# Moving the probability scaling of sparse attention to GpSimd, cutting weight splitting into pieces, and starting the gate products behind the compressed scores

## The reference, cut to what matters

```python
def masked_softmax(s, mask):
    s = jnp.where(mask, s.astype(jnp.float32), NEG_INF)
    return jax.nn.softmax(s, axis=-1) * mask
...
        o_cmp, p_cmp = nsa_compressed(q, kv[:, :, 0], kv[:, :, 1], ...)   # 31 compressed keys
...
    out = lax.map(body, (qb, ib, mb, jnp.arange(nq)))                     # selected and window keys
...
        y = (gm[:, :, 0] * (y_nsa @ w_proj_nsa[l]) + gm[:, :, 1] * (y_ml @ w_proj_ml[l])
             + gm[:, :, 2] * (y_mem @ w_proj_mem[l]))
```

## Time and profile before

| | us |
|---|---|
| median of 3 runs | 2846.68 (2845.8 to 2847.77) |
| the profiled execution's own time | 2845.7 |
| its span | 2843.9 |
| PE busy | 2756.7 (97%) |
| DVE busy | 2074.1 (73%) |
| ACT busy | 1194.7 (42%) |
| POOL busy | 86.9 (3%) |

### The profile page before, as it was taken

The page is one execution under the profiler, slowest core; times in us unless marked ns, Lnnn a source line. Parts: engine busy times, 40 slices in busy tenths (PEclk is TensorE's granted clock), DMA queues, the critical chain, the costliest instruction groups (busy, mean ns, idle before and its releaser), DMA issues.

```text
span 2843.9 us, 41346 instructions
## 1 busy us (share of the span) xinstructions
PE 2756.7 (97%) x16318; PEld 2421.5 (85%) x16318; DVE 2074.1 (73%) x3097; ACT 1194.7 (42%) x1739; POOL 86.9 (3%) x114
## 2 busy tenths in 40 slices
PE   7999898899999999999999999999999999999998
PEld 7888777777888989889898899987999888789897
DVE  4456567676658969589695797875978588669794
ACT  4333455555333434334343444332434357524342
POOL 0000022221000000000000000000000000000000
PEclk9999999999999999999999999999999999999999
DMA  7223313222533332323333233332332343123332
GB/s 221 89 78 104 111 53 93 78 93 84 171 119 104 112 111 95 128 75 115 108 97 98 81 107 109 97 98 91 101 116 93 109 174 121 60 74 104 108 100 74
DMA packets 262207, 295.51 MB, mean 104 GB/s; under 512 B 6210, under 2 KB 248018, under 8 KB 259342
## 3 DMA queue, kind: packets, MB, share of 16 engines
q1 hardware_dynamic: 257008, 281.53, 30.6%
q10 hardware_dynamic: 5022, 11.57, 1.1%
HBM read 276.30 MB, written 16.78 MB: 103 GB/s over the span
## 4 chain that ended last, share of the span: by engine, by line
PE 86%; DVE 8%; issue 3%; ACT 2%; ACTq 0%; DVEq 0%; DMA 0%; SPq 0%
PE bank L1461 14%; PE bank L1462 14%; PE bank L1463 14%; PE bank L1898 8%; PE bank L1896 8%; PE bank L1897 8%; PE bank L1735 3%; PE bank L2059 1%; PE bank L1476 1%; PE bank L1477 1%; PE bank L1478 1%; PE bank L1803 1%; PE bank L1754 1%; DVE probT_low L2451 1%; PE bank L1489 1%
## 5 line engine op out<-in xcount | busy, mean ns | idle before, releaser
L2154 DVE TENSOR_TENSOR w_lo<-w_raw,w_hi 128x2048 fp32r<-128x2048 f32 (+2 forms) x140 | 306.3, 2190 | 139.0 <-ACT w_hi L847 134.1
L847 ACT ACTIVATE w_hi<-w_raw 128x2048 fp32r<-128x2048 f32 (+2 forms) x134 | 243.0, 1820 | 240.9 <-PE bank L1463 162.2
L1461 PE MATMUL bank<-hid_hi,w_hi 128*128 128x512 f32 x880 | 343.0, 390 | 0.0
L1462 PE MATMUL bank<-hid_lo,w_hi 128*128 128x512 f32 x880 | 342.5, 389 | 0.0
L1463 PE MATMUL bank<-hid_hi,w_lo 128*128 128x512 f32 x880 | 342.4, 389 | 0.0
L1461 PE MATMUL bank<-h_hi,w_hi 128*128 128x512 f32 x752 | 298.8, 397 | 3.4 <-DVE w_lo L2154 1.7
L1462 PE MATMUL bank<-h_lo,w_hi 128*128 128x512 f32 x752 | 293.1, 390 | 0.0
L1463 PE MATMUL bank<-h_hi,w_lo 128*128 128x512 f32 x752 | 293.0, 390 | 0.0
L1463 PEld LDWEIGHTS bank<-hid_hi,w_lo 128*128 128x128 f32 x880 | 165.2, 188 | 34.5
L1461 PEld LDWEIGHTS bank<-hid_hi,w_hi 128*128 128x128 f32 x880 | 165.2, 188 | 34.0
L1462 PEld LDWEIGHTS bank<-hid_lo,w_hi 128*128 128x128 f32 x880 | 165.2, 188 | 33.6
(11 more groups left out here) (479 smaller groups left out, 7060.6 us busy)
## 6 DMA issues: line engine op xcount, KB each, us to landing
w_raw<-in_ffn_w_in_dram SPq DMA_DIRECT2D x88, 1024.0 KB, 5.1
w_raw<-in_ffn_w_out_dram SPq DMA_DIRECT2D x32, 1024.0 KB, 5.0
w_raw<-in_w_in_dram SPq DMA_DIRECT2D x28, 1024.0 KB, 5.2
w_raw<-in_w_ffn_in_dram SPq DMA_DIRECT2D x22, 1024.0 KB, 5.1
w_raw<-in_ffn_w_out_dram SPq DMA_DIRECT2D x16, 768.0 KB, 4.3
w_raw<-in_conv_w_pw_dram SPq DMA_DIRECT2D x12, 1024.0 KB, 6.3
phase_taps<-in_conv_dw_phases_dram SPq DMA_DIRECT2D x10, 1152.0 KB, 7.7
w_raw<-in_w_ffn_down_dram SPq DMA_DIRECT2D x8, 1024.0 KB, 5.0
```

The lines of the kernel that those rows point to most:

```text
L847: nc.scalar.activation(w_hi[SLOT[u]][:, 0:n], raw[s][:, 0:n], ACT.Copy).then_inc(w_hi_ready, 1)
L1461: nc.tensor.matmul(bank[b][:, 0:n], wh, xh, start=first, stop=False)
L1462: nc.tensor.matmul(bank[b][:, 0:n], wh, xl, start=False, stop=False)
L2154: v.tensor_tensor(w_lo[slot][:, 0:n], raw[s][:, 0:n], w_hi[slot][:, 0:n].bitcast(F32), ALU.subtract).then_inc(w_lo_ready, 1)
```

## The change

It does six things, all in the loop over the groups or at its start. (1) Each item's probabilities are multiplied by one over the sum and by the gate on POOL, in one instruction per head with two factors from columns (`normalise` in the `gpsimd` block); DVE keeps only the reciprocal (`invert_sums`, which signals `s_r`) and once a group copies the gates to one place (`group_gates`). (2) POOL's weight splitting is dealt out in pieces of 256 columns behind its items (`LOW_PIECES`). (3) ACT's conversions of weights move to rounds 9, 14, 18 and 19 (`HIGH_AT`), the last one in two halves. (4) For the query block of 128 keys the high part of the turned probabilities is made by DVE, not ACT. (5) Four gate products stand between the compressed scores and the first scores, rounds 0 and 1 have 10 each and all others 6; the sum is still 144. (6) The compressed sums and gain are made in round 3, the value split in round 4; and DVE's first signal to `y_split` stands at the very start of its program.

```diff
+GATE_FIRST = 4
+GATE_ITEM = [10, 10] + [6] * 20
 GATE_EVAC = {}
 for _m in range(5):
-    GATE_EVAC[min(_q for _q in range(NI + 2) if sum(GATE_ITEM[0:_q + 1]) >= 3 * KT * (_m + 1))] = _m
+    GATE_EVAC[min(_q for _q in range(NI + 2) if GATE_FIRST + sum(GATE_ITEM[0:_q + 1]) >= 3 * KT * (_m + 1))] = _m
 N_PROB = 5
+HIGH_AT = (9, 14, 18, 19)
+LOW_PIECES = {0: ((0, 4, 6),), 1: ((0, 6, 8),), 9: ((1, 0, 2),), 10: ((1, 2, 3),), 11: ((1, 3, 4),),
+              14: ((2, 0, 2),), 15: ((2, 2, 3),), 16: ((2, 3, 4),), 19: ((3, 0, 8),)}
...
-NSA_PER = 49
+NSA_PER = 19
...
-        cg = nst[:, 160:192]
+        gate_now = nst[:, 160:208].rearrange("p (q h b) -> p q h b", h=HPG, b=3)
...
+            def half_high_in_loop(u2, s, slot, half):
+
+                if half == 0:
+                    act.wait_ge(w_landed[s], u2 * 16 + 16)
+                    act.wait_ge(w_used, u2 * 2 + (s - 1))
+                part = slice(HALF * half, HALF * (half + 1))
+                ins = nc.scalar.activation(w_hi[slot][:, part], raw[s][:, part], ACT.Copy)
+                if half == 1:
+                    ins.then_inc(w_hi_ready, 1)
...
                     n = P * (qb + 1)
+                    if qb == 0:
+                        return
...
                         gate_evac(GATE_EVAC[q])
-                        if GATE_EVAC[q] == 1:
-                            high_in_loop(g * 2 + (U_NSA // 2 + 1), 0, 0, HALF)
-                        if GATE_EVAC[q] == 3:
-                            high_in_loop(g * 2 + (U_NSA // 2 + 1), 1, 1, HALF)
-                        if GATE_EVAC[q] == 4:
-                            high_in_loop(g * 2 + (U_NSA // 2 + 2), 0, 0)
+                    if q == HIGH_AT[0]:
+                        high_in_loop(g * 2 + (U_NSA // 2 + 1), 0, 0, HALF)
+                    if q == HIGH_AT[1]:
+                        high_in_loop(g * 2 + (U_NSA // 2 + 1), 1, 1, HALF)
+                    if q in HIGH_AT[2:]:
+                        half_high_in_loop(g * 2 + (U_NSA // 2 + 2), 0, 0, HIGH_AT.index(q) - 2)
...
-            def low_in_loop(u, s, n=UNIT):
-
-                pool.wait_ge(w_hi_ready, u + 1)
-                for c in range(0, n, UC):
+            def low_pieces(u, s, first, last, n):
+
+                if first == 0:
+                    pool.wait_ge(w_hi_ready, u + 1)
+                for c in range(first * UC, last * UC, UC):
                     ins = nc.gpsimd.tensor_tensor(w_lo[s][:, c:c + UC], raw[s][:, c:c + UC], w_hi[s][:, c:c + UC].bitcast(F32), ALU.subtract)
-                ins.then_inc(w_lo_ready, 1)
+                if last * UC == n:
+                    ins.then_inc(w_lo_ready, 1)
...
-                for n in range(4):
-                    if n == 1:
-                        pool.wait_ge(c_gain, g + 1)
+                def normalise(q):
+
+                    qb, br, pr = ITEMS[q]
+                    n = P * (qb + 1)
+                    pool.wait_ge(s_r, g * (NS // 2) + (STEP_OF[q] // 2 + 1))
+                    pool.sem_inc(s_open, 1)
+                    for h in range(2):
+                        i = STEP_OF[q] + h
+                        nc.gpsimd.tensor_scalar(prob[i % N_PROB][:, 0:n], prob[i % N_PROB][:, 0:n], prec[:, i:i + 1],
+                                                gate_now[:, qb, 2 * pr + h, br + 1:br + 2], ALU.mult, ALU.mult).then_inc(s_n, 1)
+
+                low_pieces(g * 4 + (U_NSA + 1), 1, 0, 4, UNIT)
+                for q in range(NI):
+                    if ITEMS[q][1] != CMP:
+                        normalise(q)
+                    if q == 3:
                         nc.gpsimd.tensor_tensor(pc3, pc3, cg_c.unsqueeze(2).to_broadcast([P, 16, NC]), ALU.mult).then_inc(c_p, 1)
-                    low_in_loop(g * 4 + (U_NSA + 1 + n), (n + 1) % 2, HALF if n in (1, 2) else UNIT)
+                    for n, first, last in LOW_PIECES.get(q, ()):
+                        low_pieces(g * 4 + (U_NSA + 1 + n), (n + 1) % 2, first, last, HALF if n in (1, 2) else UNIT)
...
-                pe.wait_ge(kd_landed, g * 128 + 128)
-                pe.wait_ge(evac_act, NFIX)
-                pe.wait_ge(evac_dve, DVE_EVACS[NFIX])
...
+                gates(GATE_FIRST)
+                pe.wait_ge(kd_landed, g * 128 + 128)
+                pe.wait_ge(evac_act, NFIX)
+                pe.wait_ge(evac_dve, DVE_EVACS[NFIX])
                 scores_of(0)
...
             chain = Chain(dve_chain_s)
+            dve.sem_inc(y_split, 2)
             v = nc.vector
...
-            dve.sem_inc(y_split, 2)
             link(v.memset(vc_st[:, :].bitcast(F32), 0.0))
...
-                between = {0: (cmp_max, cmp_shift), 4: (cmp_sum, cmp_gain, split_cmp_values), 9: (lambda: compressed_keys(g + 1),)}
+                def group_gates():
+                    link(v.tensor_copy(gate_now, gate4[:, :, bass.ds(g * HPG, HPG), :]))
+
+                between = {0: (cmp_max, cmp_shift, group_gates), 3: (cmp_sum, cmp_gain), 4: (split_cmp_values,), 9: (lambda: compressed_keys(g + 1),)}
...
-                def normalise(q):
-
-                    qb, br, pr = ITEMS[q]
-                    i, n = STEP_OF[q], P * (qb + 1)
-                    two = slice(i, i + 2)
+                def invert_sums(q):
+
+                    i = STEP_OF[q]
                     dve.wait_ge(s_e, g * NS + (i + 2))
-                    link(v.reciprocal(prec[:, two], psum_row[:, two]))
-                    link(v.tensor_tensor(cg[:, two], prec[:, two], gate4[:, qb, bass.ds(g * HPG + 2 * pr, 2), br + 1], ALU.mult))
-                    for h in range(2):
-                        p_ = prob[(i + h) % N_PROB][:, 0:n]
-                        v.tensor_scalar(p_, p_, cg[:, i + h:i + h + 1], None, ALU.mult).then_inc(s_n, 1)
+                    v.reciprocal(prec[:, i:i + 2], psum_row[:, i:i + 2]).then_inc(s_r, 1)
...
+                    for h in range(2):
+                        if qb == 0:
+                            dve.wait_ge(s_t, g * NT + TURN_OF_STEP[STEP_OF[q] + h])
+                            v.tensor_scalar(probT[0][:, h, 0:n], bank[5 + h][:, 0:n], 1.0, None, ALU.mult).then_inc(s_pa, 1)
...
-                        normalise(q - 1)
+                        invert_sums(q - 1)
```

5 lines of the change are left out of this document (2 added, 3 removed).

## The result

The changed kernel took 2831.29 us (median of 5 runs, 2828.87 to 2834.93), the kernel before beside it 2845.80 (2844.13 to 2847.77). The ratio is 0.9948, 95% interval 0.9933 to 0.9962: 14.5 us faster, where 19.3 were forecast. 2831.3 lies in the range of 2808 to 2842. In the series of the experiments the kernel before shows two levels of time, 2844 to 2851 us and, in 22 of 58 executions, 2854 to 2859 at a slightly lower mean granted clock, so that its median there, and each ratio to it, depends on how many executions fell on the upper one.

The account below looks back on a forecast made before the run. PE, busy 97% of the span, was taken as the bound, so only its waits or low-clock work could be won. 14.4 from rounds plus 6.3 less 1.4 at starts: 19.3 us, 2845.7 to 2826.4; range 2818 to 2834, eight in ten 2808 to 2842.

Parts of the forecast that it names:

- The start of the first group: With DVE's signal given at program start, the first transposes go at 366.1 instead of 372.4: 6.3 us won, once.
- The rounds: Item rounds 2 to 21 of each group: gains and losses sum to about 3.6 us won, 14.4 over four groups.
- rounds 19 to 21: End of a group: DVE makes the high part, conversions come in halves, POOL scales before splitting; 10.4 becomes 7.4, won 3.0.
- round 7: ACT's conversion with a gate tile ahead of it is gone from round 6: 5.4 becomes 3.9 us, won 1.5.
- rounds 2 to 4: Softmax ahead of item 1's low parts, value split ahead of item 2's: 13.7 becomes 14.7 us, lost 1.0.
- The price of the multiply: POOL's multiply by two column factors, taken from the nearest row: 1.05 us at 512 columns, 0.41 at 128.
- Rival (a): Multiply cheap, 0.65 us at 512 columns: PE's waits on POOL vanish in most rounds, 2810 us; 20 in 100.
- rival (c): Multiply slow: each 0.1 us in PE's wait costs 3.8 us; decides from 1.72 us at 512 columns; 6 in 100.
- the one on the queries: Next group's queries land 5.0 to 9.5 us after asking, needed 9.3 later: only slowest landing shows, 0.2 us, nothing.
- The three later starts: Starts of the other three groups: two extra gate products delay each one's transposes 0.46 us, 1.4 us in all.
- (b): Only the first start is won; item rounds lose to POOL's latency what they gain on DVE: 2841 us; 13 in 100.
- (d): DVE and POOL get in each other's way, some 10 us of loss at most: 2836 us; 9 in 100.

Follow-up runs that it names:

- start_alone: The kernel before with only DVE's signal to y_split moved to the program's start: 2840.51 us, ratio 0.9966.
- multiply_twice: The changed kernel with POOL's multiply made in two steps, by 1/sum and then by the gate: 2898.47 us, ratio 1.0162.
- softmax_back: The changed kernel with the softmax over the compressed keys back in round 4 on DVE, together with the value split: 2821.77 us, ratio 0.9901.
- pieces_in_fours: The changed kernel with POOL's weight splitting dealt out in fewer, longer runs: 2828.76 us, ratio 0.9914.
- queries_first: The changed kernel with SP asking for the next group's queries ahead of the second weight load: 2828.26 us, ratio 0.9923.
- after_again: The changed kernel run once more without an edit: 2828.76 us, ratio 0.9926.
- merge_half: The changed kernel with PE's first merge products waiting for POOL's first four pieces of a weight unit, not all eight: 2827.96 us, ratio 0.9926.
- scale_on_dve: The changed kernel with the multiplies by 1/sum and gate back on DVE, in the two-factor form: 2840.40 us, ratio 0.9970.
- act_part_back: The changed kernel with the next unit's conversion in one piece in round 17 and the last rows' high parts on ACT: 2840.18 us, ratio 0.9962.
- better: The changed kernel with queries ahead of the second weight load, a finer signal before the merge, and other gate-product numbers per round: 2825.34 us, ratio 0.9916.

## Why the prediction was right, and where its terms were off

**The start of the first group** was right: 6.27 us won (366.14 against 372.41), 6.3 said. start_alone shows the cause.

**The rounds** were right in sum: 3.73 us a group against 3.6. By their terms, second group, forecast and measured: rounds 19 to 21 won 3.0 and 2.42; round 7 won 1.5 and 1.48; round 10 lost 0.55 and 0.72; rounds 2 to 4 lost 1.0 and 0.37; rounds 9, 12, 14 and 15 won 1.4 and 1.24; the others, which are eight and not nine, lost 0.8 and 0.32.

**Two of those terms hide wrong steps that met each other.** The price of the multiply was 1.05 us; it measured 0.77. By the sentence that each 0.1 us is worth 3.8 us this should have given 10.6 us more, about 2816, and it did not. At 0.77 PE meets a tensor that is just ready, or nearly: it idles at most 0.3 us for POOL at a round's start. Above that, multiply_twice shows 8.4 us for each 0.1. The step should have drawn a corner near the measured price and no line through both ends. By that slope a multiply of 1.05 us, as priced, would have cost up to 23 us, more than the whole gain; that is an estimate, and no run has this price. That the rounds came out near is luck: the two errors have opposite signs. Rival (a), 2810 for a cheap multiply, expected from a lower price what 0.77 instead of 1.05 did not give (no run has its 0.65), and rival (c) had its mechanism right and its point of decision too far off.

**The step on rounds 2 to 4** compared the new order with the old one and found the loss of round 3, but it took the shorter round 4 to be bought with it. softmax_back shows that with the scaling off DVE round 4 has room for both. I had not asked which gap the moved work leaves behind, and what it would cost to stay.

**The step that failed** is the one on the queries: "only the slowest landing shows, 0.2 us: nothing". It had the time from issue to need nearly right (8.8 us, forecast 9.3), but took the landing times of before, with a second weight load that was issued 5 us ahead. That load waits for POOL's last piece of the slot, which the change moves behind the scalings of round 16; I followed the query load and not what stands ahead of it on SP. Cost in this execution: 2.8 us (round 21 of the first group), in another 1.6. pieces_in_fours and queries_first each remove it in their own way.

**The three later starts** were to lose 1.4 us together and lost 2.8 here, 0.2 in after_again. What changes is how long each start stays at the low clock: in these two traces a start took 13.8 to 14.5 us with 3.4 us at the low clock, 15.9 to 16.0 with 6.8 and 17.2 with 10.2; before, each took 14.7 with 6.8. With the 6.8 us at the low clock that the old start had, the new one is 0.6 to 1.3 us longer in the traces of this order, and not 0.46 as forecast.

**A wait was missing from the sum**: PE's 1.25 us ahead of the merge. POOL's eight pieces begin when its last scaling is done and take 5.6 us; merge_half removes it.

In all, over the loop: 6.3 and four times 3.73 won, 2.8 lost at the starts, 2.8 to the queries, 1.35 ahead of the merge, is 14.2, and the first merge product stands at 684.45 instead of 698.71. Of the rivals, (b) is out, since the rounds are won and scale_on_dve and act_part_back each lose about 10 us or more; of (d) the contention is there (below), and what it costs the rounds in all no run shows.

**What stays open**: why the clock falls at one start and not at the next of the same program. A wait of PE ahead of it (3.0 us in the changed kernel) goes with the earliest fall, but with no wait at all (queries_first, better, pieces_in_fours) it fell in every later start; in softmax_back, with a wait of 1.0 us ahead of one of the three, in that one alone; and in multiply_twice, without a wait, in two of the three.

## What to carry to other kernels

When work moves to a slower engine, follow what that engine then finishes later (here the last piece of a split) through every queue that waits for it, down to the loads behind it, and look for two large transfers that come to leave together. Price a wait as a corner: cheap while the waiting engine has work of its own, then at full slope for each instruction in the chain; and find on which side the price lies. When a change consists of several moves, ask of each what it costs to leave it where it was in the new order, not in the old one: one of the moves here cost 5 us in the rounds and was worth nothing.

## What the runs showed of the hardware

POOL's multiply by two column factors takes 0.34 us and 0.84 ns a column (447 ns at 128, 769 at 512), while its subtraction of two tensors takes 739 ns at 256. The Trainium skill, "GPSIMD Engine Reference", section 4.1, says that GpSimd takes about twice VectorE's time with two inputs and roughly the line rate with one; by the slope, at the 1.2 GHz of the prediction's estimate, the rows agree, and that estimate of 0.65 us was short by a larger fixed part (0.34 us and not 0.2). With one factor instead of two it took 0.70.

DVE and POOL still get in each other's way on short operations. The CAST of 31x128 took 0.22 us in softmax_back with POOL idle. In the changed kernel it took 0.70 while POOL was scaling, by the timelines of DVE and of POOL:

```profile
462.08 0.70 DVE L2446 CAST v_cmp_parts<-v_cmp_parts 31x128 fp32r<-31x128 f32 x1
```

```profile
461.93 1.52 POOL L1460 TENSOR_SCALAR prob<-prob,nsa_stat 128x512 f32<-128x512 f32 x2 [2.35 <-DVE nsa_stat L2469]
```

Likewise the product of 16 columns at L2440 took 0.67 in softmax_back beside POOL, 0.18 in the changed kernel without it, while the reduction at L2432 took 0.67 with POOL at work beside nearly all of it and 0.65 with POOL beside half of it. The product just ahead of it, L2439, took 0.18 in both kernels, in softmax_back too, where it ran as POOL went from one multiply to the next; so not every such operation is held up. The Trainium skill, "SBUF — State Buffer", section "Who interferes with whom", has operations with two SBUF inputs contend with GpSimd, casts where they run in a two-port mode, and reductions on trn2 never. The rows on the cast and on the product at L2440 agree; of the reduction there is no run with POOL idle.
